# Memory norm, keys and values before the input's products, and the long convolution's tiles handed out in another order

## The chip, the core and the metric

The kernel runs on one core of one Trainium2 chip. The metric is the device time of one execution in microseconds (us). Besides it there is a profile of one execution, whose span runs from the first to the last instruction.

## The reference

Two transformer blocks are applied one after the other to 256 positions of width 1024, all in float32. Only the first part of the first block matters here.

```
h     = rmsnorm(x) * norm_mix_g                     # x: 256 x 1024
p_a, p_b, q, p_g = split(h @ w_in)                  # w_in: 1024 x 9216
y_a   = (gb * causal_conv3(gc * v)) @ w_a_out       # gb, gc, v = split(p_a)
u     = u * sigmoid(ug)                             # u, ug = split(p_b)
u     = silu(layernorm(causal_conv31(u) + bias))    # 31 taps for each of 1024 channels
y_b   = u @ w_b_out
k, vm = split((rmsnorm(mem) * norm_mem_g) @ w_kv)   # mem: 256 x 1024, w_kv: 1024 x 2048
y_c   = attention(q, k, vm) @ w_att_out             # 4 heads of 256
out   = (sigmoid(p_g0)*y_a + sigmoid(p_g1)*y_b + sigmoid(p_g2)*y_c) @ w_o
```

The feed-forward part and the whole second block follow. They are the same in both kernels.

## The kernel before

Everything is one program with five instruction streams, each written out by hand and each executed in its order: SyncE (weight loads), GpSimd, ScalarE, VectorE and TensorE. They meet only at counted semaphores.

**Slots.** A weight matrix is read in pieces of 1 MB (128 x 2048 float32). A piece is here called a slot. Each is split into an upper and a lower part: ScalarE copies `raw` to `whi` (line 489, the helper `hi`), VectorE subtracts, `wlo = raw - whi` (line 843, the helper `lo`), and TensorE multiplies in three passes (line 1317): upper by upper, upper by lower, lower by upper. There are three buffers (`R = 3`), so slot g+3 can be loaded when `lo(g)` is done, and `hi(g+3)` can run when TensorE has used slot g (`slot_used`). TensorE starts slot g when `lo(g)` is done (`lo_ready`).

**Stages of the first 345 us.** Slots 0 to 11 are `ugq` (u, its gate ug and the attention's queries q, three slots a round, four rounds), 12 to 19 are `kv` (four slots of keys by `to_channels`, four of values by `to_rows`), 20 to 31 are `cvb` (for branch a, four rounds of three), 32 to 43 are `gate` (four rounds of three), and 44 on are `a_out`. Below, u1 to u12, kv1 to kv8, c1 to c12 and g1 to g12 are the slots of these stages in order. The variable `G_KV` and its like hold the first slot of a stage. `USES` counts how often each of the eight PSUM banks was read before a stage.

**Norms.** A norm takes squares on ScalarE (line 499), statistics on VectorE and GpSimd, a scaling on VectorE (line 862), 16 transposes on TensorE (line 1364, which write PSUM banks 0 to 3), and the split of the result (ScalarE `norm_upper`, VectorE `norm_lower`). `n_mix` is the norm of `x`, `n_mem` that of `mem`. Before, `n_mix` comes first, and `n_mem` runs during `ugq`; its transposes and split stand between `ugq` and `kv`. There too stand three transposes of `cwf_rows`, copied out by ScalarE (line 594).

**The long convolution.** Its eight tiles of 128 channels are shared: VectorE does tiles 0 to 5, GpSimd tiles 6 and 7. VectorE's share of a tile is cut into four parts of 7 or 8 taps (line 965, one instruction a tap; a first part has two copies more, a last part one addition). The parts stand between the `lo` of the slots: before, two in round 2 and two in round 3 of `ugq` (tile 0), one behind each `lo` of `kv` (tiles 1 and 2), one in each round of `cvb` (tile 3), two in each round of `gate` (tiles 4 and 5). Tile c can begin when round c//2 of `ugq` has given u (`glu`). GpSimd takes two instructions a tap (lines 426 and 430), 31 taps a tile, and begins when both norms are transposed (`norm_tr` is 8), since its scratch is the norms' buffer `xn`, and when `glu` says that tiles 6 and 7 are there.

**A round of `cvb` on VectorE** (`branch_a`): a product (line 1003), a `lo`, the three-tap convolution (lines 1014 and 1017), a `lo`, a product (line 1022), and then a `lo` whose `hi` stands on ScalarE behind a copy of that product's result (line 616):

```
                act.wait_ge(bank_read[2], USES["cvb"][2] + 1 + i)
                nc.scalar.activation(q_hi[:, bass.ds(BW * i, BW)], work[:, 1860:2372], ACT.Copy).then_inc(an_hi, 1)
                hi(G_CVB + 5, i)
```

Then a lower part (line 1025) and the round's part of the long convolution follow.

Of the kernel before, what the change touches and what calls it, by code (L numbers as in the profile page):

```python
# [18 lines left out]
ACT = mybir.ActivationFunctionType  # L19
# [14 lines left out]
CONV_DVE = 6  # L34
# [22 lines left out]
G_UGQ, G_KV, G_CVB, G_GATE, G_AO, G_ATT, G_BO, G_WO = 0, 12, 20, 32, 44, 48, 52, 56  # L57
# [15 lines left out]
    ("setup", {0: 1}), ("n_mix", LOW4), ("ugq", {1: 4, 2: 4}), ("setup2", {3: 1}), ("n_mem", LOW4),  # L73
    ("kv", {**LOW4, **HIGH4}), ("cvb", {0: 4, 1: 4, 2: 4}), ("gate", {0: 4, 1: 4, 2: 4}),
# [22 lines left out]
NORMS = ["n_mix", "n_mem", "n_ffn", "fin1", "n_mix2a", "n_ffn2a", "n_mix2b", "n_ffn2b", "fin2"]  # L97
TNORMS = ["n_mix", "n_mem", "n_ffn", "n_mix2a", "n_ffn2a", "n_mix2b", "n_ffn2b"]
TGAIN = [V_MIX, V_MEM, V_FFN, V_MIX2, V_FFN2, V_MIX2 + 1, V_FFN2 + 1]


def two_blocks(nc, d, out):
    with ExitStack() as ctx:
# [176 lines left out]
        def _(sp):  # L280
            x_rows = d["x"].rearrange("(t p) n -> p t n", p=P)
            for t in range(T):
                sp.dma_start(x[:, t, :], x_rows[:, t, :]).then_inc(x_in[t], 16)

# [14 lines left out]
            for j, c0 in enumerate((3 * D, 4 * D, 5 * D)):  # L299
                load(G_UGQ + j, cols("w_in", c0), KD)  # L300
            with sp.Fori(1, 4) as i:
                for j, c0 in enumerate((3 * D, 4 * D, 5 * D)):
                    load(G_UGQ + j, cols("w_in", c0 + 256 * i), KD, i)
            for i in range(4):
                load(G_KV + i, cols("w_kv", 256 * i), KD)
            for i in range(4):
                load(G_KV + 4 + i, d["w_kv"].rearrange("(k p) n -> p k n", p=P)[:, 2 * i:2 * i + 2, D:2 * D], 2)
# [53 lines left out]
        def _(pool):  # L361
# [55 lines left out]
            for c in range(CONV_DVE, KD):  # L417
                pool.wait_ge(glu, 2 + c // 2)
                dst = conv[:, c * S:(c + 1) * S]
                for k in range(K_B):  # L420
                    src, w = misc[:, c * UP + k:c * UP + k + S], gain(V_CONVB + k, c)
                    if k == 0:
                        nc.gpsimd.tensor_scalar(dst, src, w, gain(V_CBIAS, c), ALU.mult, ALU.add).then_inc(pool_tap, 1)
                    else:
                        tap = xn[:, 0, S * (k % 2):S * (k % 2) + S]
                        nc.gpsimd.tensor_scalar(tap, src, w, None, ALU.mult).then_inc(pool_mul, 1)  # L426
                        steps += 1
                        pool.wait_ge(pool_mul, steps)
# [50 lines left out]
        def _(act):  # L479
# [89 lines left out]

            act.dma_start(vec_rows, d["vecs"]).then_inc(vec_in, 16)  # L570
            act.dma_start(mem_rows, d["mem"].rearrange("(t p) n -> p t n", p=P)).then_inc(mem_in, 16)
            squares("n_mix", x, lambda b: act.wait_ge(x_in[b // 2], 16))
# [4 lines left out]
            norm_upper("n_mix", p_hi)  # L577
# [3 lines left out]
            squares("n_mem", mem_rows, lambda b: act.wait_ge(mem_in, 16))  # L581
# [11 lines left out]
            act.wait_ge(vec_tr, 2)  # L593
            nc.scalar.activation(cwf[:, :], bank(3, 0, K_F * FT), ACT.Copy).then_inc(bank_read[3], 1)
            norm_upper("n_mem", q_hi)

            for i in range(4):
                act.wait_ge(slot_used, G_KV + i + 1)
                nc.scalar.activation(kreg[:, BW * i:BW * (i + 1)], bank(i), ACT.Copy).then_inc(bank_read[i], 1)
                hi(G_KV + i + 3)  # L600
            for i in range(4):
                if i == 3:
                    act.wait_ge(slot_used, G_KV + 8)
                    for b in range(4):
                        nc.scalar.activation(v_tok[:, b // 2, BW * (b % 2):BW * (b % 2) + BW], bank(4 + b),
                                             ACT.Copy).then_inc(bank_read[4 + b], 1)
                hi(G_KV + 7 + i)

# [226 lines left out]
        def _(dve):  # L835
# [106 lines left out]
            normalise("n_mix", x)  # L942
            norm_lower("n_mix", p_hi, p_lo)
            lo(0)
            lo(1)
            lo(2)

# [25 lines left out]
            def ugq(i, parts=()):  # L973
# [7 lines left out]
                for part in parts[:1]:  # L981
                    conv_part(0, 0, part, 2)
                lo(G_UGQ + 5, i)
                for part in parts[1:]:
                    conv_part(0, 0, part, 2)

            ugq(0)
            normalise("n_mem", mem_rows)
            ugq(1, (0, 1))
            ugq(2, (2, 3))  # L990
            ugq(3)
            norm_lower("n_mem", q_hi, q_lo)
# [35 lines left out]
            for i in range(4):  # L1028
                branch_a(i)
                conv_part(3, 3 * TAPS, i, 3)  # L1030
            for i in range(4):
                for j in range(3):
                    lo(G_GATE + 3 + j, i)
                    if j:
                        c = 4 + i // 2
                        conv_part(c, c * TAPS, 2 * (i % 2) + j - 1, 4)
# [274 lines left out]
        def _(pe):  # L1311
# [145 lines left out]
            transpose_norm("n_mix")  # L1457
            phases = (("ugq", G_UGQ), ("cvb", G_CVB), ("gate", G_GATE))

            def memory():  # L1460

                pe.wait_ge(cwf_in, 16)
                for k in range(K_F):
                    last = nc.tensor.transpose(bank(3, FT * k, FT * (k + 1)), cwf_rows[:, P * k:P * k + P],
                                               ident[0:FT, 0:FT])
                last.then_inc(vec_tr, 1)
                pe.wait_ge(glu, 5)
                transpose_norm("n_mem")
                for i in range(4):
                    free(i, USES["kv"][i])  # L1470
                    to_channels(G_KV + i, i, q_pair, 0, "n_mem" if i == 0 else None)
                for i in range(4):
                    to_rows(G_KV + 4 + i, 2, q_pair, 2 * i, 4, 2, BW, i == 0, i == 3)
# [23 lines left out]
            pe.wait_ge(conv_tap, (K_B + 3) * CONV_DVE)  # L1497
            pe.wait_ge(pool_tap, K_B * (KD - CONV_DVE))
# [195 lines left out]
```

## Time and profile before

| | us |
|---|---|
| time, median of 3 runs | 1332.91 (1332.78 to 1339.92) |
| span of the profiled execution | 1326.9 |
| median of the runs less that span | 6.0 |
| TensorE busy in the span | 1207.3 (91%) |
| VectorE busy | 856.2 (65%) |
| ScalarE busy | 619.5 (47%) |
| GpSimd busy | 310.5 (23%) |
| weight split on VectorE (line 843), 189 instructions | 440.2 |
| taps on VectorE (line 965), 174 instructions | 89.9 |

The profiled execution has no time of its own beside its span. Busy shares are means over stages with different limits, so a stage is read from its own rows: which engine the others wait for, and for how long. In a row of the timeline, the numbers are the start, the length, the engine, the line, the operation and the tiles; the bracket at the end is the idle time ahead of it and what ended that. "x8" is eight instructions, drawn as one.

### The profile page before, as it was taken

The numbers are of one execution on the slowest core, as the hardware profiler recorded it, in microseconds if no ns is written. First come the engines' busy times: TensorE is split into PE (matmuls) and PEld (weight loads), VectorE is DVE, ScalarE is ACT, GpSimd is POOL, SyncE is SP. The second block draws the span as 40 slices with busy tenths as digits, with TensorE's granted clock in tenths as the row PEclk, the third lists the DMA queues.
The fourth block names the chain that finished last, engine by engine and source line by source line (L and its number), as shares of the span: only waits on it lengthen the run. The fifth ranks groups of instructions, "written<-read, shape, count | busy, mean of one in ns | idle before, by whom it ended". The sixth has DMA issues, their size and how long they took to land.

```text
span 1326.9 us, 20560 instructions
## 1 busy us (share of the span) xinstructions
PE 1207.3 (91%) x8039; PEld 1116.8 (84%) x8039; DVE 856.2 (65%) x1099; ACT 619.5 (47%) x834; POOL 310.5 (23%) x301
## 2 busy tenths in 40 slices
PE   5989899999799899999677889999989988899997
PEld 5989789999798899998566769999979777799996
DVE  4678988887566666667568846555554485655554
ACT  5553323444444444444457634444444474444442
POOL 1009999601300100000113405870000140000000
PEclk8999999999799899999888899999999979999999
DMA  8553444555136455554233027555545502355550
GB/s 261 176 184 115 140 151 154 189 190 190 32 128 192 150 190 188 180 181 147 83 131 127 1 96 200 188 190 190 190 128 189 190 1 94 129 191 190 185 189 37
DMA packets 139431, 201.00 MB, mean 151 GB/s; under 512 B 3258, under 2 KB 119994, under 8 KB 139376
## 3 DMA queue, kind: packets, MB, share of 16 engines
q1 hardware_dynamic: 138128, 195.83, 44.9%
q0 software_dynamic: 912, 3.17, 1.1%
q10 hardware_dynamic: 336, 1.25, 0.3%
q8 instruction: 36, 0.59, 0.2%
q14 instruction: 19, 0.16, 0.0%
HBM read 199.19 MB, written 1.05 MB: 151 GB/s over the span
## 4 chain that ended last, share of the span: by engine, by line
PE 74%; DVE 17%; ACT 5%; issue 2%; POOL 1%; DMA 1%; POOLq 0%; ACTq 0%; SPq 0%
PE ps L1317 68%; DVE wlo L843 5%; DVE work L965 4%; PE ps L1378 4%; ACT whi L489 2%; ACT xn L499 1%; PE ps L1364 1%; PE ps L1414 1%; DVE work L926 1%; DVE work L1017 1%; ACT p_hi L509 1%; DMA x<-in_x 1%; DVE stat L916 1%; POOL q_lo L383 0%; DVE x L884 0%
## 5 line engine op out<-in xcount | busy, mean ns | idle before, releaser
L843 DVE TENSOR_TENSOR wlo<-raw,whi 128x2048 fp32r<-128x2048 f32 x189 | 440.2, 2332 | 248.7 <-ACT whi L489 248.3
L1317 PE MATMUL ps<-p_hi,whi 128*128 128x256 f32 x1632 | 467.6, 287 | 21.5 <-DVE wlo L843 17.6
L1317 PE MATMUL ps<-p_lo,whi 128*128 128x256 f32 x1632 | 465.8, 285 | 0.0
L1317 PE MATMUL ps<-p_hi,wlo 128*128 128x256 f32 x1632 | 465.5, 285 | 0.0
L489 ACT ACTIVATE whi<-raw 128x2048 fp32r<-128x2048 f32 x189 | 361.3, 1914 | 187.0 <-PE ps L1317 187.0
L1317 PEld LDWEIGHTS ps<-p_hi,whi 128*128 128x128 f32 x1632 | 317.1, 194 | 26.7 <-DVE wlo L843 19.9
L1317 PEld LDWEIGHTS ps<-p_lo,whi 128*128 128x128 f32 x1632 | 317.2, 194 | 1.5
L1317 PEld LDWEIGHTS ps<-p_hi,wlo 128*128 128x128 f32 x1632 | 317.2, 194 | 0.0
L377 POOL TENSOR_TENSOR stat<-stat 128x1 f32<-128x1 f32 x18 | 14.8, 822 | 647.1 <-DVE stat L851 647.1
L1317 PE MATMUL ps<-whi,q_hi 128*128 128x512 f32 x376 | 148.0, 394 | 3.6 <-DVE wlo L843 2.0
L1317 PE MATMUL ps<-whi,q_lo 128*128 128x512 f32 x376 | 147.6, 392 | 0.0
L1317 PE MATMUL ps<-wlo,q_hi 128*128 128x512 f32 x376 | 146.8, 390 | 0.0
L965 DVE SCALAR_TENSOR_TENSOR work<-work 128x256 f32<-128x256 f32 x174 | 89.9, 586 | 0.0
L1317 PEld LDWEIGHTS ps<-whi,q_hi 128*128 128x128 f32 x376 | 71.1, 189 | 18.9 <-DVE wlo L843 2.9
L1317 PE MATMUL ps<-whi,p_hi 128*128 128x512 f32 (+2 forms) x196 | 77.0, 393 | 10.6 <-DVE p_lo L1188 3.9
L426 POOL TENSOR_SCALAR xn<-misc,vec 128x256 f32<-128x256 f32 x60 | 85.5, 1425 | 0.0
L1317 PEld LDWEIGHTS ps<-wlo,q_hi 128*128 128x128 f32 x376 | 71.0, 189 | 15.2
L1317 PEld LDWEIGHTS ps<-whi,q_lo 128*128 128x128 f32 x376 | 71.2, 189 | 13.2
L1317 PE MATMUL ps<-wlo,p_hi 128*128 128x512 f32 (+2 forms) x196 | 76.4, 390 | 0.0
L1317 PE MATMUL ps<-whi,p_lo 128*128 128x512 f32 (+2 forms) x196 | 76.3, 389 | 0.0
L779 ACT ACTIVATE work<-ps 128x512 f32<-128x512 f32 x32 | 19.1, 597 | 120.0 <-PE ps L1317 120.0
L430 POOL TENSOR_TENSOR misc<-misc,xn 128x256 f32<-128x256 f32 x60 | 64.5, 1075 | 5.0
(209 smaller groups left out, 1560.2 us busy)
## 6 DMA issues: line engine op xcount, KB each, us to landing
raw<-in_w_in SPq DMA_DIRECT2D x36, 1024.0 KB, 5.0
raw<-in_w_up SPq DMA_DIRECT2D x22, 1024.0 KB, 5.1
raw<-in_up_a SPq DMA_DIRECT2D x16, 1024.0 KB, 5.4
raw<-in_down_a SPq DMA_DIRECT2D x16, 1024.0 KB, 4.9
raw<-in_up_b SPq DMA_DIRECT2D x16, 1024.0 KB, 5.4
raw<-in_down_b SPq DMA_DIRECT2D x16, 1024.0 KB, 4.9
raw<-in_od_w_qkv SPq DMA_DIRECT2D x12, 1024.0 KB, 5.1
raw<-in_w_down SPq DMA_DIRECT2D x11, 1024.0 KB, 4.9
```

The source lines that it names most:

```text
L377: nc.gpsimd.tensor_tensor(out=rr[:, c:c + 1], in0=ms[:, c:c + 1], in1=mhalf[:, 0:1], op=ALU.pow).then_inc(norm_r, 1)
L426: nc.gpsimd.tensor_scalar(tap, src, w, None, ALU.mult).then_inc(pool_mul, 1)
L430: nc.gpsimd.tensor_tensor(out=dst, in0=dst, in1=tap, op=ALU.add).then_inc(pool_tap, 1)
L489: nc.scalar.activation(whi[:, g % R, :], raw[:, g % R, :], ACT.Copy).then_inc(hi_ready, 1)
L499: last = nc.scalar.activation(xn[:, t, half], src[:, t, half], ACT.Square, accum_out=ss[:, T * n + t, m:m + 1])
L509: nc.scalar.activation(dst[:, c * S:(c + 1) * S], bank(c // 2, c % 2 * S, c % 2 * S + S), ACT.Copy, scale=gain(TGAIN[m], c)).then_inc(norm ...
L779: nc.scalar.activation(work[:, 0:BW], bank(slot), ACT.Relu).then_inc(f2_r, 1)
L843: nc.vector.tensor_tensor(wlo[:, g % R, :], raw[:, g % R, :], whi[:, g % R, :].bitcast(F32), ALU.subtract).then_inc(lo_ready, 1)
L916: nc.vector.tensor_scalar(att_nmax[:, pair], att_max[:, pair], -1.0 if biased else -scale(i), None, ALU.mult).then_inc(at_nm, 1)
L965: nc.vector.scalar_tensor_tensor(out=acc[k % 2], in0=src, scalar=w, in1=acc[k % 2], op0=ALU.mult, op1=ALU.add).then_inc(conv_tap, 1)
L1317: ins = nc.tensor.matmul(dst, lhs, rhs, start=first and n == 0, stop=last and n == 2)
L1378: ins = nc.tensor.matmul(dst, a, b, start=first and n == 0, stop=last and n == 2)
```

## The change

The memory's part comes first. SyncE loads three slots of `w_kv`, then `x`, then the rest of `w_kv`, and only then `w_in`; ScalarE's queue loads `mem` ahead of the vectors. The first norm is `n_mem`, slots 0 to 7 are `kv`, and 8 to 19 are `ugq`. The norm of `x` is computed during kv1 to kv4, and its transposes stand behind kv4, with those of `cwf_rows` ahead of them. `cvb` and `gate` keep their slot numbers 20 to 43.

The convolution's tiles are handed out anew: GpSimd takes tiles 0 and 1, VectorE tiles 2 to 7. VectorE's 24 parts are taken from a list in order: one in round 2 of `ugq`, three each in rounds 3 and 4, two in each round of `cvb`, and one behind each of the first nine `lo` of `gate`. None stands in `kv`.

```diff
-CONV_DVE = 6
+CONV_POOL = 2
...
-G_UGQ, G_KV, G_CVB, G_GATE, G_AO, G_ATT, G_BO, G_WO = 0, 12, 20, 32, 44, 48, 52, 56
+G_KV, G_UGQ, G_CVB, G_GATE, G_AO, G_ATT, G_BO, G_WO = 0, 8, 20, 32, 44, 48, 52, 56
...
         @block.sync
-            for t in range(T):
-                sp.dma_start(x[:, t, :], x_rows[:, t, :]).then_inc(x_in[t], 16)
...
-            for j, c0 in enumerate((3 * D, 4 * D, 5 * D)):
-                load(G_UGQ + j, cols("w_in", c0), KD)
-            with sp.Fori(1, 4) as i:
+            for i in range(3):
+                load(G_KV + i, cols("w_kv", 256 * i), KD)
+            for t in range(T):
+                sp.dma_start(x[:, t, :], x_rows[:, t, :]).then_inc(x_in[t], 16)
+            load(G_KV + 3, cols("w_kv", 256 * 3), KD)
+            for i in range(4):
+                load(G_KV + 4 + i, d["w_kv"].rearrange("(k p) n -> p k n", p=P)[:, 2 * i:2 * i + 2, D:2 * D], 2)
+            with sp.Fori(0, 4) as i:
                 for j, c0 in enumerate((3 * D, 4 * D, 5 * D)):
                     load(G_UGQ + j, cols("w_in", c0 + 256 * i), KD, i)
...
         @block.gpsimd
             pool.wait_ge(norm_tr, 8)
-            for c in range(CONV_DVE, KD):
+            for c in range(CONV_POOL):
                 pool.wait_ge(glu, 2 + c // 2)
...
         @block.scalar
             def squares(name, src, ready=None):
                 n = NORMS.index(name)
+                if name == "n_mix":
+                    act.wait_ge(norm_tr, 4 * TNORMS.index("n_mem") + 4)
...
+            act.dma_start(mem_rows, d["mem"].rearrange("(t p) n -> p t n", p=P)).then_inc(mem_in, 16)
             act.dma_start(vec_rows, d["vecs"]).then_inc(vec_in, 16)
-            act.dma_start(mem_rows, d["mem"].rearrange("(t p) n -> p t n", p=P)).then_inc(mem_in, 16)
-            squares("n_mix", x, lambda b: act.wait_ge(x_in[b // 2], 16))
+            squares("n_mem", mem_rows, lambda b: act.wait_ge(mem_in, 16))
...
-            norm_upper("n_mix", p_hi)
+            norm_upper("n_mem", q_hi)
             hi(0)
             hi(1)
             hi(2)
-            squares("n_mem", mem_rows, lambda b: act.wait_ge(mem_in, 16))
+            squares("n_mix", x, lambda b: act.wait_ge(x_in[b // 2], 16))
+            for i in range(4):
+                act.wait_ge(slot_used, G_KV + i + 1)
+                nc.scalar.activation(kreg[:, BW * i:BW * (i + 1)], bank(i), ACT.Copy).then_inc(bank_read[i], 1)
+                hi(G_KV + i + 3)
+            act.wait_ge(vec_tr, 2)
+            nc.scalar.activation(cwf[:, :], bank(3, 0, K_F * FT), ACT.Copy).then_inc(bank_read[3], 1)
+            norm_upper("n_mix", p_hi)
+            for i in range(4):
+                if i == 3:
+                    act.wait_ge(slot_used, G_KV + 8)
+                    for b in range(4):
+                        nc.scalar.activation(v_tok[:, b // 2, BW * (b % 2):BW * (b % 2) + BW], bank(4 + b),
+                                             ACT.Copy).then_inc(bank_read[4 + b], 1)
+                hi(G_KV + 7 + i)
...
         @block.vector
-            normalise("n_mix", x)
-            norm_lower("n_mix", p_hi, p_lo)
+            normalise("n_mem", mem_rows)
+            norm_lower("n_mem", q_hi, q_lo)
             lo(0)
             lo(1)
             lo(2)
+            normalise("n_mix", x)
+            for i in range(4):
+                lo(G_KV + 3 + i)
+            norm_lower("n_mix", p_hi, p_lo)
+            for i in range(4, 8):
+                lo(G_KV + 3 + i)
...
+            parts_left = [(c, part) for c in range(CONV_POOL, KD) for part in range(4)]
+
+            def conv_parts(count):
+                for _ in range(count):
+                    c, part = parts_left.pop(0)
+                    conv_part(c, (c - CONV_POOL) * TAPS, part, 2 + c // 2)
+
+            def ugq(i, count):
                 lo(G_UGQ + 3, i)
...
                 lo(G_UGQ + 4, i)
-                for part in parts[:1]:
-                    conv_part(0, 0, part, 2)
+                conv_parts(count // 2)
                 lo(G_UGQ + 5, i)
-                for part in parts[1:]:
-                    conv_part(0, 0, part, 2)
-
-            ugq(0)
-            normalise("n_mem", mem_rows)
-            ugq(1, (0, 1))
-            ugq(2, (2, 3))
-            ugq(3)
-            norm_lower("n_mem", q_hi, q_lo)
-            for i in range(8):
-                lo(G_KV + 3 + i)
-                conv_part(1 + i // 4, TAPS * (1 + i // 4), i % 4, 3)
+                conv_parts(count - count // 2)
+
+            ugq(0, 0)
+            ugq(1, 1)
+            ugq(2, 3)
+            ugq(3, 3)
...
             for i in range(4):
                 branch_a(i)
-                conv_part(3, 3 * TAPS, i, 3)
+                conv_parts(2)
             for i in range(4):
                 for j in range(3):
                     lo(G_GATE + 3 + j, i)
-                    if j:
-                        c = 4 + i // 2
-                        conv_part(c, c * TAPS, 2 * (i % 2) + j - 1, 4)
+                    conv_parts(min(len(parts_left), 1))
...
         @block.tensor
             last.then_inc(vec_tr, 1)
+            transpose_norm("n_mem")
+            phases = (("ugq", G_UGQ), ("cvb", G_CVB), ("gate", G_GATE))
+
+            for i in range(4):
+                free(i, USES["kv"][i])
+                to_channels(G_KV + i, i, q_pair, 0, "n_mem" if i == 0 else None)
+            free(3, USES["setup2"][3])
+            pe.wait_ge(cwf_in, 16)
+            for k in range(K_F):
+                last = nc.tensor.transpose(bank(3, FT * k, FT * (k + 1)), cwf_rows[:, P * k:P * k + P],
+                                           ident[0:FT, 0:FT])
+            last.then_inc(vec_tr, 1)
             transpose_norm("n_mix")
...
+            for i in range(4):
+                to_rows(G_KV + 4 + i, 2, q_pair, 2 * i, 4, 2, BW, i == 0, i == 3)
             ready_low("n_mix")
...
                 if phase == "cvb":
-                    memory()
+                    pe.wait_ge(glu, 5)
```

## Rows read from the trace of the kernel before

**Rows 1.** busy time of each engine in two stretches, us from the start

```profile
core 0: us, PE busy (x) PEld busy (x) DVE busy (x) ACT busy (x) POOL busy (x), PEclk, DMA share, GB/s
98.00:147.00 49.00, 46.93 (x287) 42.01 (x288) 42.52 (x56) 16.48 (x15) 47.25 (x43) 0.97 0.38 129
147.00:231.00 84.00, 74.37 (x580) 72.73 (x580) 76.14 (x93) 28.09 (x23) 81.41 (x64) 0.96 0.46 150
```

**Rows 2.** chain of work that ended last: start, length, what

```profile
20.53 71.28 PE ps L1317 x576
...
97.99 6.12 PE ps L1317 x48
...
250.18 70.87 PE ps L1317 x576
```

**Rows 3.** TensorE in order of time: the first product after a wait

```profile
147.96 0.38 PE L1317 MATMUL ps<-p_hi,whi 128*128 128x256 f32 x1 [0.52 <-DVE wlo L843]
...
211.26 0.39 PE L1317 MATMUL ps<-p_hi,whi 128*128 128x256 f32 x1 [2.46 <-DVE wlo L843]
...
230.66 0.38 PE L1317 MATMUL ps<-p_hi,whi 128*128 128x256 f32 x1 [0.39 <-DVE wlo L843]
...
250.18 0.58 PE L1317 MATMUL ps<-p_hi,whi 128*128 128x256 f32 x1 [1.99 <-DVE wlo L843]
```

**Rows 4.** VectorE in order of time, rounds of the `cvb` loop

```profile
168.43 2.28 DVE L843 TENSOR_TENSOR wlo<-raw,whi 128x2048 fp32r<-128x2048 f32 x1
...
188.95 2.27 DVE L843 TENSOR_TENSOR wlo<-raw,whi 128x2048 fp32r<-128x2048 f32 x1
...
203.51 4.89 DVE L965 SCALAR_TENSOR_TENSOR work<-work 128x256 f32<-128x256 f32 x8
...
208.93 2.28 DVE L843 TENSOR_TENSOR wlo<-raw,whi 128x2048 fp32r<-128x2048 f32 x1
...
216.27 0.68 DVE L1022 TENSOR_TENSOR work<-ps,work 128x512 f32<-128x512 f32 x1
...
219.55 2.29 DVE L843 TENSOR_TENSOR wlo<-raw,whi 128x2048 fp32r<-128x2048 f32 x1 [2.60 <-ACT whi L489]
...
228.33 2.28 DVE L843 TENSOR_TENSOR wlo<-raw,whi 128x2048 fp32r<-128x2048 f32 x1
```

**Rows 5.** VectorE in order of time, GpSimd idle (first row) and working

```profile
63.05 3.25 DVE L965 SCALAR_TENSOR_TENSOR work<-work 128x256 f32<-128x256 f32 x8
...
121.94 2.84 DVE L843 TENSOR_TENSOR wlo<-raw,whi 128x2048 fp32r<-128x2048 f32 x1
...
139.96 0.30 DVE L955 COPY work<-misc 128x286 f32<-128x286 f32 x1
...
145.63 2.28 DVE L843 TENSOR_TENSOR wlo<-raw,whi 128x2048 fp32r<-128x2048 f32 x1
```

**Rows 6.** GpSimd in order of time: first and last of its taps

```profile
96.83 0.55 POOL L423 TENSOR_SCALAR misc<-misc,vec 128x256 f32<-128x256 f32 x1 [50.30 <-PE ps L1364]
...
98.37 0.74 POOL L430 TENSOR_TENSOR misc<-misc,xn 128x256 f32<-128x256 f32 x1
...
100.10 0.73 POOL L430 TENSOR_TENSOR misc<-misc,xn 128x256 f32<-128x256 f32 x1
...
253.12 0.73 POOL L430 TENSOR_TENSOR misc<-misc,xn 128x256 f32<-128x256 f32 x1
```

**Rows 7.** ScalarE in order of time: the start, the pace of the slots

```profile
8.33 0.63 ACT L499 ACTIVATE xn<-x 128x512 f32<-128x512 f32 x1 [1.41 <-DMA x<-in_x]
...
28.48 1.91 ACT L489 ACTIVATE whi<-raw 128x2048 fp32r<-128x2048 f32 x1 [1.22 <-PE ps L1317]
...
126.94 1.92 ACT L489 ACTIVATE whi<-raw 128x2048 fp32r<-128x2048 f32 x1 [3.12 <-PE ps L1317]
...
132.38 1.92 ACT L489 ACTIVATE whi<-raw 128x2048 fp32r<-128x2048 f32 x1 [3.52 <-PE ps L1317]
```

**Rows 8.** the tile `merged`, which the load of `mem` writes

```profile
L571 ACTq DMA_DIRECT2D merged<-in_mem x1: 443/443/443, 1.2 to 1.2; - x1
...
DMA to landing us min/median/max: 9.3/9.3/9.3
```

More of the change, by code:

```diff
@@ L72 @@
 PHASES = [
-    ("setup", {0: 1}), ("n_mix", LOW4), ("ugq", {1: 4, 2: 4}), ("setup2", {3: 1}), ("n_mem", LOW4),
-    ("kv", {**LOW4, **HIGH4}), ("cvb", {0: 4, 1: 4, 2: 4}), ("gate", {0: 4, 1: 4, 2: 4}),
+    ("setup", {0: 1}), ("n_mem", LOW4), ("kv", {**LOW4, **HIGH4}), ("setup2", {3: 1}), ("n_mix", LOW4),
+    ("ugq", {1: 4, 2: 4}), ("cvb", {0: 4, 1: 4, 2: 4}), ("gate", {0: 4, 1: 4, 2: 4}),
     ("a_out", LOW4), ("att1", {2: 2, 3: 2, **HIGH4}), ("att_out", LOW4), ("b_out", LOW4),
@@ L95 @@
 USES = earlier_bank_uses()
-NORMS = ["n_mix", "n_mem", "n_ffn", "fin1", "n_mix2a", "n_ffn2a", "n_mix2b", "n_ffn2b", "fin2"]
-TNORMS = ["n_mix", "n_mem", "n_ffn", "n_mix2a", "n_ffn2a", "n_mix2b", "n_ffn2b"]
-TGAIN = [V_MIX, V_MEM, V_FFN, V_MIX2, V_FFN2, V_MIX2 + 1, V_FFN2 + 1]
+NORMS = ["n_mem", "n_mix", "n_ffn", "fin1", "n_mix2a", "n_ffn2a", "n_mix2b", "n_ffn2b", "fin2"]
+TNORMS = ["n_mem", "n_mix", "n_ffn", "n_mix2a", "n_ffn2a", "n_mix2b", "n_ffn2b"]
+TGAIN = [V_MEM, V_MIX, V_FFN, V_MIX2, V_FFN2, V_MIX2 + 1, V_FFN2 + 1]
 def two_blocks(nc, d, out):
@@ L297, in rows @@
                 return d[w].rearrange("(k p) n -> p k n", p=P)[:, bass.ds(k0, kk), :]
-            for j, c0 in enumerate((3 * D, 4 * D, 5 * D)):
-                load(G_UGQ + j, cols("w_in", c0), KD)
-            with sp.Fori(1, 4) as i:
+            for i in range(3):
[6 more added lines that the diff above has]
+            with sp.Fori(0, 4) as i:
                 for j, c0 in enumerate((3 * D, 4 * D, 5 * D)):
                     load(G_UGQ + j, cols("w_in", c0 + 256 * i), KD, i)
[L304 to L307, printed above, removed]
             with sp.Fori(1, 5) as i:
@@ L592, in _ @@
                 hi(G_UGQ + 5, i)
[L593 to L607, printed above, removed]
             with act.Fori(0, 4) as i:
@@ L971, in conv_part @@
                         in1=acc[1], op0=ALU.add, op1=ALU.add).then_inc(conv_tap, 1)
-            def ugq(i, parts=()):
+            parts_left = [(c, part) for c in range(CONV_POOL, KD) for part in range(4)]
[4 more added lines that the diff above has]
+            def ugq(i, count):
                 lo(G_UGQ + 3, i)
@@ L1456, in _ @@
             last.then_inc(vec_tr, 1)
-            transpose_norm("n_mix")
[L1458 to L1473, printed above, removed]
+            transpose_norm("n_mem")
[9 more added lines that the diff above has]
+            last.then_inc(vec_tr, 1)
+            transpose_norm("n_mix")
+            for i in range(4):
+                to_rows(G_KV + 4 + i, 2, q_pair, 2 * i, 4, 2, BW, i == 0, i == 3)
             ready_low("n_mix")
@@ L1496, in _ @@
                 to_channels(G_AO + i, i, q_pair)
[L1497 to L1498 removed]
+            pe.wait_ge(conv_tap, (K_B + 3) * (KD - CONV_POOL))
+            pe.wait_ge(pool_tap, K_B * CONV_POOL)
             free(7, USES["att1"][7])
```

## The prediction

> **What bounds the kernel now.** I read the busy times by stretch first. From 98 to 147 us (`kv`) and from 147 to 231 us (`cvb`) TensorE is busy nearly throughout, but VectorE is too: 42.5 of 49 and 76.1 of 84 us, with GpSimd at 47 of 49 and 81 of 84 [rows 1]. Which of the two leads is told by the chain of waits. It runs through TensorE alone from 20.53 us for 12 slots of `ugq` (71.28 us) and again from 250.18 us for 12 slots (g4 to the third of `a_out`, 70.87 us) [rows 2]. Between 97.99 and 250 us it runs mostly through VectorE. TensorE's own rows agree: its waits there end with a `wlo` of VectorE, 2.46 us ahead of c10 and 1.99 us ahead of g4 [rows 3].
>
> TensorE's pace when nothing holds it: slot u1 takes 20.53 to about 28.45 (ScalarE's copy for the next one starts at 28.48 [rows 7]), 7.9 us, and the other eleven 5.77 each [rows 2]. A row slot of `kv` takes 132.38 - 126.94 = 5.44 us [rows 7]. A round of three slots is 17.3 us.
>
> VectorE's pace in a round of `cvb` is the distance of its first `wlo`: 168.43, 188.95, 208.93, 228.33, that is 20.52, 19.98 and 19.40 us [rows 4]. In each stands one part of the long convolution. Beside GpSimd's work a part of 8 taps takes 4.85 us (203.51 to 208.4 [rows 4]) and a first part 5.67 us (139.96 to 145.63 [rows 5]). Without the part the rounds are 14.85, 15.1 and 14.55, mean 14.85. This holds 2.6 us in which VectorE waits for ScalarE (216.27 + 0.68 to 219.55 [rows 4]); what stands behind that wait can't fill it. So a `cvb` round is over TensorE's 17.3 us already with one part.
>
> **What the change does to it.** Neither the 44 slots nor the 24 parts on VectorE nor the 62 taps on GpSimd change in number. Only their places do: 4, 8, 4 and 8 parts in `ugq`, `kv`, `cvb` and `gate` become 7, 0, 8 and 9. I follow the new order from the start, with the durations above.
>
> Start. The first squares now want `mem`. Before, the second half of `x` let them start at 8.33 [rows 7]; `mem` was issued at 1.2 us and took 9.3 us beside `x` and the vectors [rows 8]. It goes first now, but all four squares (two of 0.63 us more) come behind it. Below: nothing, if it lands in the time of half a load. Above: issued at 0.7, it lands at 10.0, 1.7 us later than `x`, plus 1.3 of squares: 3 us. It has the lead over only the 1 MB of `w_kv`, so I take 0.5: TensorE starts at 21.0.
>
> `kv`. Slots kv1 to kv4: 7.9 + 3 x 5.77, to 46.2 us. Then bank 3 must be copied, a `hi` stands ahead of the copy of the `cwf` transposes, and the 16 transposes of `n_mix` follow. Before, the same chain and the lower split made TensorE go from 91.8 to 97.99 [rows 2], 6.2 us. The split is no longer waited for; I take 4.4 (ends: 3 and 6.2). Its cover is that `wlo` of kv5 to kv7 are done by then, and that the norm's squares, statistics and scaling run beside kv1 to kv4, where VectorE has 2.3 of each 5.8 us to do. kv5 to kv8 are 21.7 us: `ugq` starts at 72.3. Before, `kv` was paced by VectorE (a `lo` of 2.75 and a part of 4.85 make 7.6 us a slot).
>
> `ugq`. u1 to u10 run at 5.77, u11 and u12 too. GpSimd starts when round 1 gives u, about 14.2 us in, at 86.5 (before 96.83 [rows 6]). The parts: `lo(u9)` ends at 111.7, the first part at 117.4, `lo(u10)` 119.9, the product for u and `lo(u11)` 124.7, a part 129.5, `lo(u12)` 132.3, two parts 142.0, `lo(c1)` 144.6, the last product of u 145.3. TensorE has used u12 at 141.5 and waits for that product ahead of `cvb`: c1 starts at 145.3. Before it started at 147.96 [rows 3]. That is the whole gain: 2.7 us.
>
> `cvb`. VectorE goes on: `lo(c2)` 148.0, a first part 153.7, `lo(c3)` 156.4, two parts 166.1, the product 166.7, `lo(c4)` 169.0. TensorE, done with c3 at 162.6, starts c4 there. From c4 to c7 to c10 to g1 VectorE has 14.85 us and two parts each: 4.9 + 5.7, 4.85 + 4.85, 4.9 + 5.7. The sum is 25.45 + 24.5 + 25.45 = 75.4 us, against 3 x 17.3 on TensorE. g1 starts at 244.4. Before it was 230.66 [rows 3]. `cvb` takes 99.1 us from c1 to g1 instead of 82.7.
>
> `gate`. GpSimd's taps took 96.83 to 253.85, 157 us [rows 6]; from 86.5 on they end near 241 to 244, just as g1 starts. From there a part costs 3.25 [rows 5] and a `lo` 2.2. The last `cvb` round then needs from `lo(g1)` on: 2.7 of taps of branch a, 2.2, 0.7, 2.6 of waiting, 2.2, 1.0, two parts 6.4, and `lo(g4)` 2.2: 20.0 us, g4 at 264.4 (before 250.18). After that a slot costs VectorE 5.5 us on the mean, less than 5.77, so TensorE leads. Its 12 slots take 69.6 us (before 70.87, behind a longer wait), to 334.0. Before they ended at 250.18 + 70.87 = 321.05.
>
> Sum: -2.7 to c1, +16.4 in `cvb`, +0.5 in g1 to g3, -1.3 in the 12 slots: +12.9 us. From there on everything is as before. Against the profiled span that is 1326.9 + 12.9 = 1339.8; the median of the runs lies 6.0 above the span, so 1332.9 + 12.9 = 1345.8, say 1346 us, 1.0% more.
>
> The waits of 6 to 7 us ahead of c4, c7, c10 and g1 may also leave TensorE at its lower clock for the first slot behind them, as in u1 (7.9 for 5.77). This costs nothing: a round has 25 us for 17.3 + 2.1.
>
> The price of a part beside GpSimd is the term that matters. The row says that 8 taps go from 3.25 to 4.89 us [rows 4, 5], and a `wlo` from 2.29 to 2.84. The Trainium skill ("SBUF — State Buffer", section "SBUF: two separate sides") states instead that VectorE with two SBUF inputs and GpSimd lock a shared pair of ports for a whole instruction and the other fully blocks. By that rule a tap of 0.41 us would stand behind a GpSimd instruction of 0.73 or more each time, 1.14 us, and a part would cost 9.1 us; the four added in `cvb` would cost 36 us instead of 19.8. The trace does not agree for these forms: its part takes 4.89.
>
> **Rivals.** (a) *VectorE is relieved in time; faster.* GpSimd's tap step is 1.73 us where VectorE is idle (98.37 to 100.10 [rows 6]), 107 us for 62. In the new order VectorE is nearly idle until 111.7. If GpSimd were done near its 107 us, at 194, the two last long rounds would cost 1.6 us less for each part and some 1.5 less for the rest, about 4.7 each, the contended half round before it some 2, and the last parts of `cvb` too: 11 to 12 us back and g1 at 233, and with contention cheaper in rounds 1 and 2 besides (7 us at most) the time would be 1326 to 1334. Its point of decision: GpSimd's end must be before about 195 us. Against it: 157 - 107 = 50 us of its time were lost beside VectorE's instructions, and all but the first 25 us lie beside just such work. Chance 0.05.
>
> (b) *Part of this only; no change or little.* GpSimd ends near 225, or the parts fill waits better than I think, and 6 to 10 us come off: 1336 to 1340. For it: the free start. Chance 0.13, half of it within 0.5%.
>
> (c) *The change does not move the bound.* If `ugq` and `cvb` were paced by TensorE all the same, the end would come from 72.3 + 36 x 5.77 = 280.0 + 17.3 = 297.4 instead of 321.05: 1309 us. Against it are the 19.4 us rounds with a single part. Chance 0.02.
>
> (d) *`gate` stays behind.* If GpSimd lasts to 260, the last `cvb` round and the first five `gate` slots stay at 7.0 to 7.6 us each: 5 + 5 to 8 us more, 1353 to 1358. For it: two parts a round meet it longer. Chance 0.1.
>
> (e) *The start and the break behind kv4 cost their upper ends*: 2.5 + 1.8 us more, 1350. This lies in my forecast's own range.
>
> (f) *The lock.* 13 parts beside GpSimd at 4.3 us more than now: 1400. The row of before, which holds 12 such parts, speaks against it: chance 0.01.
>
> **How the numbers follow.** My forecast has 0.69: own range 1341 to 1352, from the terms that I rounded (start and break -1.5 to +4.3, GpSimd's end by 10 us earlier -3, the base of a round 14.55 to 15.1, so -1 to +1). A measurement of this kernel can tell some 0.5%, 6.7 us, from no change, that is 1326.2 to 1339.6. Faster: (c) and half of (a), with a little for what I can't see, 0.06. Same: the rest of (a) and half of (b), 0.09. Slower: 0.85. The range that leaves out (a), (c), (f) and the far parts of (b) and (d): 1337 to 1354.
>
> **What would show it.** Right: `kv` from 21 to 72 us without a wait but one of some 4 us behind its fourth slot; GpSimd's first tap at 86 and its last near 242; VectorE's first `wlo` of a `cvb` round 24.5 to 25.5 us apart; TensorE waiting 6 to 8 us for it each time, four times; no long wait behind g4; a first score near 334. Wrong: rounds under 22 us, which would mean that a part is cheap beside GpSimd or that GpSimd is done; waits on `wlo` deep in `gate` (rival d); a later start than 23; or a change behind 345 us, which none of my steps allows.

## The result, and the profile after

| | before | changed |
|---|---|---|
| time, median | 1334.4 us (4 runs) | 1350.6 us (1347.3 to 1355.2, 4 runs) |
| ratio, 95% interval | | 1.0122, 1.0064 to 1.0180 |
| span of the profiled execution | 1326.9 | 1349.1 |
| third slot of `a_out` ends | 321.05 | 335.30 |

The change makes the kernel 1.2% slower. The second timing, below, gives 1.0099 (1.0071 to 1.0127). Both intervals leave out 1, and both lie below 2%. The forecast was 1346 us.

Busy time by stretch. These answer to [rows 1]:

```profile
core 0: us, PE busy (x) PEld busy (x) DVE busy (x) ACT busy (x) POOL busy (x), PEclk, DMA share, GB/s
98.00:147.00 49.00, 46.42 (x387) 46.22 (x386) 38.66 (x43) 26.55 (x20) 47.33 (x41) 1.00 0.45 150
148.00:246.00 98.00, 77.16 (x576) 76.35 (x576) 90.04 (x119) 24.36 (x18) 91.20 (x77) 0.87 0.39 129
```

In `cvb` VectorE is busy 90 of 98 us and TensorE 77. Before, the two were nearly level there (76 and 74 of 84). TensorE now plainly waits. The chain of what ended last, against [rows 2]:

```profile
0.74 7.59 DMA merged<-in_mem
...
21.81 25.28 PE ps L1319 x192
...
49.93 3.35 PE ps L1366 x16
...
53.28 68.12 PE ps L1319 x480
...
246.30 89.00 PE ps L1319 x720
```

The load of `mem` lands at 8.3 us, after which all four squares run; TensorE starts at 21.81. Behind kv4 the 16 transposes take 3.35 us. From 53.28 TensorE leads for twelve slots (four of `kv`, eight of `ugq`), and from 246.30 for fifteen, to 335.30. Between them lies VectorE. TensorE's waits, against [rows 3]:

```profile
148.52 0.38 PE L1319 MATMUL ps<-p_hi,whi 128*128 128x256 f32 x1 [4.10 <-DVE misc L989]
...
171.13 0.58 PE L1319 MATMUL ps<-p_hi,whi 128*128 128x256 f32 x1 [3.59 <-DVE wlo L841]
...
196.24 0.58 PE L1319 MATMUL ps<-p_hi,whi 128*128 128x256 f32 x1 [5.22 <-DVE wlo L841]
...
221.26 0.58 PE L1319 MATMUL ps<-p_hi,whi 128*128 128x256 f32 x1 [5.65 <-DVE wlo L841]
...
246.30 0.58 PE L1319 MATMUL ps<-p_hi,whi 128*128 128x256 f32 x1 [6.17 <-DVE wlo L841]
```

The first is c1, which waits 4.1 us for the last product of u. The others are c4, c7, c10 and g1: a wait each round, 3.6 to 6.2 us. There is none from g1 to the third slot of `a_out`. VectorE in `cvb`, against [rows 4]:

```profile
168.81 2.27 DVE L841 TENSOR_TENSOR wlo<-raw,whi 128x2048 fp32r<-128x2048 f32 x1
...
193.91 2.28 DVE L841 TENSOR_TENSOR wlo<-raw,whi 128x2048 fp32r<-128x2048 f32 x1
...
207.90 10.18 DVE L969 SCALAR_TENSOR_TENSOR work<-work 128x256 f32<-128x256 f32 x16
...
218.60 2.60 DVE L841 TENSOR_TENSOR wlo<-raw,whi 128x2048 fp32r<-128x2048 f32 x1
...
230.37 2.29 DVE L841 TENSOR_TENSOR wlo<-raw,whi 128x2048 fp32r<-128x2048 f32 x1 [2.60 <-ACT whi L487]
...
243.97 2.28 DVE L841 TENSOR_TENSOR wlo<-raw,whi 128x2048 fp32r<-128x2048 f32 x1
```

The first `wlo` of a round come at 168.81, 193.91, 218.60 and 243.97: 25.1, 24.7 and 25.4 us apart, where they were 19.4 to 20.5. Two parts stand in each round; 16 taps take 10.18 us, 0.64 each. The wait of 2.60 us for ScalarE is still there. GpSimd, against [rows 6]:

```profile
89.75 0.55 POOL L421 TENSOR_SCALAR misc<-misc,vec 128x256 f32<-128x256 f32 x1 [61.92 <-DVE misc L989]
...
241.65 0.72 POOL L428 TENSOR_TENSOR misc<-misc,xn 128x256 f32<-128x256 f32 x1
```

Its taps go from 89.75 to 242.4, 153 us, and so cover all of `cvb` but its last 4 us.

### The profile page after: what moved, and what is told of

The parts are those of the page before. It is cut to its first block, busy times and chain, and to the rows that moved or that the text cites. A ratio compares the mean times of both kernels' runs of the same rounds, so it can differ in the third digit from the quotient of the medians.

```text
span 1349.1 us, 20583 instructions
## 1 busy us (share of the span) xinstructions
PE 1222.3 (91%) x8039; PEld 1133.2 (84%) x8039; DVE 852.5 (63%) x1099; ACT 620.4 (46%) x834; POOL 306.5 (23%) x301
## 4 chain that ended last, share of the span: by engine, by line
PE 77%; DVE 14%; ACT 5%; issue 2%; DMA 1%; POOL 1%; POOLq 0%; ACTq 0%
PE ps L1319 70%; PE ps L1380 4%; DVE work L969 4%; DVE wlo L841 3%; ACT whi L487 2%; PE ps L1416 1%; PE ps L1366 1%; ACT xn L499 1%; DVE work L924 1%; DMA merged<-in_mem 1%; DVE work L1021 1%; DVE stat L911 0%; DVE stat L914 0%; DVE x L882 0%; DVE p_lo L867 0%
## 5 line engine op out<-in xcount | busy, mean ns | idle before, releaser
L1319 PE MATMUL ps<-p_hi,whi 128*128 128x256 f32 x1632 | 469.6, 288 | 29.0 <-DVE wlo L841 20.6
L1319 PEld LDWEIGHTS ps<-wlo,q_hi 128*128 128x128 f32 x376 | 70.7, 188 | 15.1
L1276 DVE TENSOR_TENSOR work<-work 128x512 f32<-128x512 f32 x32 | 22.8, 712 | 67.1 <-ACT work L777 67.1
```

The lines of the kernel that those rows point to most:

```text
L1276: nc.vector.tensor_tensor(work[:, 1024:1536], work[:, 0:BW], work[:, 0:BW], ALU.mult).then_inc(f2_sq, 1)
L1319: ins = nc.tensor.matmul(dst, lhs, rhs, start=first and n == 0, stop=last and n == 2)
```

## The experiments

Each is the kernel before or the changed one with the edit shown. "Third of `a_out`" is where the chain of waits puts the end of that slot; it tells what the first 345 us did and leaves out what follows. Medians and ratios are against the kernel before on the same chip. Its own runs went from 1321.5 to 1340.6 us, so a single span says little and the ratio counts.

| kernel | order | third of `a_out` | span | median | ratio (95%) |
|---|---|---|---|---|---|
| before | input first | 321.1 | 1326.9 | 1334 to 1336 | 1 |
| changed, again | memory first | 334.4 | 1347.3 | 1348.2 | 1.0099 (1.0071 to 1.0127) |
| tiles only | input first | 318.6 | 1330.6 | 1336.4 | 1.0011 (0.9984 to 1.0037) |
| parts to gate | memory first | 322.3 | 1328.2 | 1334.9 | 1.0012 (0.9988 to 1.0035) |
| part in the wait | memory first | 324.7 | 1334.5 | 1339.2 | 1.0040 (1.0015 to 1.0066) |
| part in the wait | input first | 313.6 | 1332.0 | 1330.6 | 0.9942 (0.9915 to 0.9970) |
| both, GpSimd kept | memory first | 315.3 | 1329.2 | 1331.2 | 0.9974 (0.9955 to 0.9994) |
| no GpSimd taps, work left out | memory first | 307.3 | 1315.3 | 1322.9 | 0.9923 (0.9890 to 0.9955) |
| all tiles on VectorE | memory first | 300.1 | 1312.2 | 1314.9 | 0.9860 (0.9832 to 0.9888) |
| all tiles on VectorE | input first | 307.4 | 1309.4 | 1321.0 | 0.9904 (0.9882 to 0.9927) |
| same, norm not held up | input first | 300.5 | 1312.6 | 1313.4 | 0.9825 (0.9780 to 0.9870) |

**1. The tiles handed out anew, alone.** The old order; GpSimd takes tiles 0 and 1, and VectorE's parts are taken from the list at their old places.

```diff
-            for c in range(CONV_DVE, KD):
+            for c in range(CONV_POOL):
                 pool.wait_ge(glu, 2 + c // 2)
...
-                conv_part(1 + i // 4, TAPS * (1 + i // 4), i % 4, 3)
+                conv_parts(1)
```

> Old order of stages, but the tiles handed out as in the change: GpSimd 0 and 1, VectorE 2 to 7, the parts at their old places. My theory (the loss is in where the parts stand, not in who does which tile): no change against the kernel before, 1333 us within 4, GpSimd's first tap again near 97 us, because it still waits for both norms' transposes. Rival (the hand-out itself costs): 5 us or more slower, with waits of TensorE in ugq or kv that were not there.

No difference that can be told (1.0011, interval 0.9984 to 1.0037). GpSimd's first tap is again at 96.85 us. So who does which tile is not the loss.

**2. Four parts moved from cvb.**

```diff
-            ugq(1, 1)
+            ugq(1, 2)
...
                 branch_a(i)
-                conv_parts(2)
+                conv_parts(1)
```

> The changed kernel with 2, 3 and 3 parts in ugq (was 1, 3, 3), one part in each cvb round (was two) and twelve in gate (was nine). My theory: cvb rounds of 19.5 to 20.5 us instead of 25; the first gate slot near 225 us instead of 246; no new wait in gate, where a slot has 5.77 us for 2.2 + 3.25; the third slot of a_out ends near 313 us (335 in the changed kernel, 321 in the one before), so 8 us faster than the kernel before, 1325. Rival (GpSimd's work reaches into gate and twelve parts there are too many): gate slots of 7 us, nothing gained over the kernel before, 1333 or more.

```profile
149.28 0.57 PE L1319 MATMUL ps<-p_hi,whi 128*128 128x256 f32 x1 [5.13 <-DVE misc L989]
...
171.88 0.39 PE L1319 MATMUL ps<-p_hi,whi 128*128 128x256 f32 x1 [3.69 <-DVE wlo L841]
...
192.50 0.39 PE L1319 MATMUL ps<-p_hi,whi 128*128 128x256 f32 x1 [1.60 <-DVE wlo L841]
...
212.47 0.39 PE L1319 MATMUL ps<-p_hi,whi 128*128 128x256 f32 x1 [2.44 <-DVE wlo L841]
```

The rounds fall to 20.6 and 20.0 us, and the waits at c7 and c10 to 1.6 and 2.4. The third of `a_out` comes at 322.3, 13 us earlier than in the changed kernel, so the doubled parts of `cvb` are the loss. It comes 9 us later than I expected (313). c4 still starts at 171.9: that place is set by the parts of `ugq`'s last round, which this edit leaves alone, and I had wrongly counted a part off there. In `gate` there is one wait of that size, 2.0 us at g4: GpSimd works until 249.2 us here, into `gate`, as the rival had it. All in all the time is that of the kernel before (1334.9), equal and not 8 us faster. This is the number that the rival named. The theory held for the rounds of `cvb`, not for what lies on either side of them.

**3. GpSimd's taps left out.** Tiles 0 and 1 of the convolution are set to zero.

```diff
             for c in range(CONV_POOL):
                 pool.wait_ge(glu, 2 + c // 2)
-                dst = conv[:, c * S:(c + 1) * S]
...
+                nc.gpsimd.memset(conv[:, c * S:(c + 1) * S], 0.0).then_inc(pool_tap, 1)
```

> The changed kernel, in which GpSimd writes zeros to tiles 0 and 1 instead of their 62 taps (those two tiles of the convolution are left out). My theory (what a part costs beside GpSimd is a third of its price): parts of 3.25 us, cvb rounds of 20 to 21 us instead of 25, first gate slot near 221 us, 24 us less than the changed kernel, 1326. Rival (the taps are slow in this stage for another reason, such as the moved loads): rounds stay at 24 to 25, 1350.

```profile
179.60 0.38 PE L1306 MATMUL ps<-p_hi,whi 128*128 128x256 f32 x1 [0.36 <-DVE wlo L828]
...
199.14 0.39 PE L1306 MATMUL ps<-p_hi,whi 128*128 128x256 f32 x1 [2.01 <-DVE wlo L828]
...
218.96 0.39 PE L1306 MATMUL ps<-p_hi,whi 128*128 128x256 f32 x1 [2.29 <-DVE wlo L828]
...
237.91 0.39 PE L1306 MATMUL ps<-p_hi,whi 128*128 128x256 f32 x1 [1.40 <-DVE wlo L828]
```

With the same parts at the same places on VectorE, 16 taps take 6.42 us, TensorE waits for VectorE neither at c1 nor at c4 (the first wait is 0.36 us, at c7), and the next rounds are 19.5, 19.8 and 19.0 us. The third of `a_out` is 28 us earlier (307.3). So beside GpSimd's taps VectorE's own work is dearer, by more than the 24 us that I expected. What GpSimd takes off VectorE is not in this run, since nobody does those two tiles; experiment 6 has both.

**4 and 5. A part in the wait for ScalarE**, in the memory-first order (the changed kernel) and in the input-first order (the kernel of experiment 1).

```diff
                 nc.vector.tensor_tensor(ca, bank(2), ca, ALU.mult).then_inc(bank_read[2], 1)
+                conv_parts(1)
                 lo(G_CVB + 5, i)
...
                 branch_a(i)
-                conv_parts(2)
+                conv_parts(1)
```

(In the input-first kernel the round's single part is the one that moves.)

> The changed kernel with one of the two parts of each cvb round put between the product of line 1026 and the lo behind it, where VectorE waits 2.6 us for ScalarE. My theory (that wait is part of VectorE's round): the wait goes, rounds of 22.4 us instead of 25.0, 10 us off over four rounds, 1340. Rival (the wait only moves, or TensorE then waits for the later lo of the third slot): rounds stay above 24, 1347 to 1350.

```profile
192.60 0.39 PE L1320 MATMUL ps<-p_hi,whi 128*128 128x256 f32 x1 [1.98 <-DVE wlo L841]
...
213.76 0.58 PE L1320 MATMUL ps<-p_hi,whi 128*128 128x256 f32 x1 [2.14 <-DVE wlo L841]
...
236.12 0.38 PE L1320 MATMUL ps<-p_hi,whi 128*128 128x256 f32 x1 [3.33 <-DVE wlo L841]
```

Rounds of 21.8, 21.2 and 22.4 us, 10.6 us less at the third of `a_out` than in the changed kernel, and a median of 1339.2: as expected.

> Old order, tiles handed out as in the change, GpSimd with its two tiles, and only the part of each cvb round moved into the wait for ScalarE. My theory: rounds of 17.3 to 17.6 us (TensorE's) instead of 19.4 to 20.5, the first gate slot near 223 us instead of 231, 7 to 9 us off, 1325 to 1328. Rival (the wait moves elsewhere): rounds above 19, 1333.

Rounds of 17.6 us: 186.94, 204.54 and 222.14 are VectorE's `wlo`. Behind c4 TensorE has no wait of 0.25 us or more in these stages. The third of `a_out` is 7.4 us earlier than in the kernel before, and 5.0 earlier than in experiment 1, which differs from this one by the moved parts alone. The time falls by 0.6%, to 1330.6, where I had expected 1325 to 1328. The 2.6 us wait was part of every round.

**6. All eight tiles on VectorE, both orders.** The tap loop of GpSimd is taken out, `CONV_POOL = 0`, 32 parts.

```diff
-            ugq(0, 0)
-            ugq(1, 1)
+            ugq(0, 2)
+            ugq(1, 3)
...
-                    conv_parts(min(len(parts_left), 1))
+                    conv_parts(2 if i == 0 and j == 0 else 1)
```

> The changed order of stages with the same two edits: VectorE does all eight tiles (11 parts in ugq, 8 in cvb, one of each round's two in the wait, 13 in gate), GpSimd none. My theory (the order itself is worth nothing either way once VectorE is not the bound): the third slot of a_out ends within 4 us of the old order with the same edits, 300 to 306, 1312 to 1319. Rival (memory first gives VectorE too little room, since eight slots have no part beside them): waits on wlo in ugq and cvb, 8 us or more behind the old order's kernel.

```profile
53.02 247.09 PE ps L1304 x1968
```

```profile
core 0: us, PE busy (x) PEld busy (x) DVE busy (x) ACT busy (x) POOL busy (x), PEclk, DMA share, GB/s
148.00:246.00 98.00, 98.00 (x819) 98.00 (x818) 97.74 (x172) 40.24 (x35) 0.00 (x0) 1.00 0.54 177
```

From 53.02 us the chain is one piece of TensorE, 247 us for 43 slots: four row slots at 5.44 and 39 at 5.77 are 246.8. VectorE is busy for 97.7 of 98 us in the middle and is waited for nowhere. 1.4% faster than the kernel before, 2.4% faster than the changed one, with a third more taps on VectorE.

VectorE's busy time from the start to the end of the third slot of `a_out`, in the kernel before (24 parts) and in this one (32 parts, memory first):

```profile
core 0: us, DVE busy (x), PEclk, DMA share, GB/s
0.00:321.05 321.05, 252.48 (x323) 0.97 0.53 174
...
0.00:300.11 300.11, 243.20 (x391) 0.99 0.56 184
```

With 62 taps more, VectorE is busy for 9 us less; input first, in the next two kernels, it is 243.7 and 243.1. Time that an instruction stands behind GpSimd counts as busy. So GpSimd's share costs VectorE more than it takes off it.

> Old order of stages; GpSimd does no tile of the long convolution, VectorE does all eight (32 parts: 8 in ugq, 8 in kv, 4 in cvb, 12 in gate), and in cvb the part stands in the wait for ScalarE. My theory (GpSimd's 62 taps cost VectorE more than they save it): parts of 3.25 us and wlo of 2.29 throughout, nearly every slot at TensorE's 5.77, the third slot of a_out ends near 299 to 303 us (321 in the kernel before), 1311 to 1317, faster than before by 1.2 to 1.6%. Rival (eight more parts are too much for VectorE, the split of work is worth its contention): waits on wlo in kv and gate, 1333 or more.

```profile
104.60 0.55 PE L1304 MATMUL ps<-q_hi,whi 128*128 128x256 f32 x1 [8.23 <-DVE q_lo L853]
```

Faster than before, but neither theory: the third of `a_out` is 307.4, not 299 to 303, and nothing waits in `kv` or `gate`. The loss is one wait of 8.2 us ahead of kv1. The two parts behind the last `lo` of `ugq` stand ahead of the memory norm's lower part on VectorE, and kv1 needs that.

**7. The same without parts in ugq's last round.**

```diff
-            ugq(3, 3)
+            ugq(3, 0)
...
                 branch_a(i)
+                conv_parts(min(i, 1))
```

> As the old order with all eight tiles on VectorE, but with no part in the last round of ugq and three more in cvb (5 in ugq, 8 in kv, 7 in cvb, 12 in gate), so that VectorE is free when the memory norm's lower part is due between ugq and kv. There TensorE waited 8.2 us with three parts in that round. My theory (the old order's weak place is that break, where the norm's last step stands on the path, and a part there comes straight on top): kv starts near 98 us again, the third slot of a_out ends 6 to 7 us earlier than with three parts there, near 297 to 299 us, and the two orders of stages are equal within 3 us, 1312 to 1316. Rival (the memory-first order is itself better, by its shorter break and nothing else in the way): 4 us or more remain behind the changed order's kernel, 1318 or more.

```profile
97.87 202.64 PE ps L1305 x1584
```

kv1 starts at 97.87 and TensorE leads to 300.5, within 0.4 us of the memory-first kernel. It is 6.9 us earlier than in the kernel with three parts there, as expected; the median is 1313.4. The intervals of the ratios, 0.9825 and 0.9860, overlap. Where VectorE is not the bound, the order of the stages is worth nothing that can be told. The order does matter in what can stand between the stages: input first, a part in the wrong place holds up a norm.

**8. Everything but GpSimd's share.** Memory first, 8 parts in `ugq`, one in each `cvb` round in the wait, 12 in `gate`, GpSimd with tiles 0 and 1.

```diff
             for c in range(CONV_POOL):
                 pool.wait_ge(glu, 2 + c // 2)
...
+            ugq(1, 2)
...
+                conv_parts(1)
                 lo(G_CVB + 5, i)
```

> The changed order with GpSimd's two tiles kept and both other repairs: 8 parts in ugq, one in each cvb round and that in the wait for ScalarE, 12 in gate. My theory (what is left against the kernel without GpSimd's taps is contention): cvb rounds of 17.3 to 17.6 us from c4 on, but c4 still near 171 (it is set by ugq's last parts), gate slots of 7 us until GpSimd ends near 245 to 250, the third slot of a_out near 313 to 317, 1326 to 1330, so 12 or more behind the kernel with all tiles on VectorE. Rival (only the places were wrong, GpSimd is no burden): within 5 us of it, 1320 or less.

The `cvb` rounds are 17.9, 17.6 and 17.6 us. The third of `a_out` is at 315.3 (57.85 us of TensorE behind a last wait at 257.49), and the median 1331.2. That slot is 15 us behind the kernel with all tiles on VectorE, which does 62 taps more there. So the places are worth 20 us against the changed kernel (335.3 to 315.3), and GpSimd's work costs another 15 with the parts at these places.

GpSimd lasts until 254.2 us, longer than expected. c4 starts at 172.6. With all tiles on VectorE it comes near 161.3, an estimate from 53.02, four slots at 5.44 and fifteen at 5.77. So 11 of the 15 us are lost by c4, beside GpSimd and the parts of the last round of `ugq`. No run keeps GpSimd's tiles and takes parts out of that round, so the smallest cost of GpSimd's share is not known.

**9. The changed kernel again.**

> The changed kernel once more, unaltered, for a second profile. The first profile lost 14 us by 335 us, and 7 to 8 more near 1110, in the third attention, where the granted clock was low for longer. My theory (that second loss is not of the change, but differs from run to run): the loss by 335 us is again 13 to 16, the stretch from 1074 to 1124 takes another length, and the median is 1346 to 1351. Rival (the second loss belongs to the change): the same 7 to 8 us near 1110 again.

The loss by the third of `a_out` is 13.3 us (14.3 in the first profile). The third attention, from its place near 1064 to 1078 us on, over 40 us in each, in the order before, changed, changed again:

```profile
core 0: us, PE busy (x), PEclk, DMA share, GB/s
1064.00:1104.00 40.00, 34.90 (x213) 0.85 0.00 1
...
1078.00:1118.00 40.00, 38.97 (x176) 0.58 0.00 1
...
1077.00:1117.00 40.00, 36.14 (x204) 0.79 0.01 2
```

The granted clock is 0.85, 0.58 and 0.79 of full speed: a mean of its two levels, 1.2 and 2.4 GHz, in unlike shares of the time, in the same code. Against the kernel before, the first profile loses 6.2 us in this attention (15.9 us behind at its start, 22.1 at its end), the second 1.4 (17.0 and 18.4). That part of the span's difference is thus not shown to be the change's.

The same goes for everything behind the third of `a_out`. The code there is the same in all twelve profiles, and it takes from 1002.0 us (all tiles on VectorE, input first) to 1018.4 (part in the wait, input first). The kernel before has 1005.9, the changed one 1013.8 and 1012.9, the tiles alone in the old order 1012.0.

## Why the prediction was right

**The mechanism.** The loss came in `cvb`, by the step that was forecast: VectorE's rounds with two parts each. The rounds were forecast at 25.45, 24.5 and 25.45 us and are 25.1, 24.7 and 25.4. GpSimd ends at 242.4 (forecast 241 to 244), but it starts at 89.75 and not at 86.5 and takes 153 us and not 157, so two errors offset each other there. `cvb` takes 97.8 us from c1 to g1 (forecast 99.1, before 82.7).

The waits of TensorE are smaller than the 6 to 8 us that I named as a sign: 3.6, 5.2, 5.7 and 6.2. In part the time went into slots at the lower clock. In the second profile c4 to c6 ran at full clock behind a wait of 3.6 us, and the wait ahead of c7 was 7.6 us and not 5.2; c7 still started 25.1 us behind c4 in both. So in `cvb` the clock costs nothing, as forecast, and the round is VectorE's.

Experiments 2 to 5 and 8 take away each factor of it: the second part, the contention, the wait for ScalarE. Rival (a) was not met: GpSimd gains only those 4 us. Of rival (b) nothing came: GpSimd does not end near 225, and the time lies above its range. Rival (c) fell with the waits at c4 to g1. Rival (d) did not happen: GpSimd was done before `gate`, and no `wlo` was waited for there. Of rival (e) the break behind kv4 came out at its upper end, 6.2 us, and the start at 0.8 of its 2.5. Rival (f) had the wrong price: beside GpSimd a tap takes 0.60 to 0.64 us on the mean, not 1.14. But the forecast was wrong to say that the trace does not agree with the rule of the lock. The single instructions, in the last section, show one engine standing behind the other; what fails is the working that made every tap stand behind a whole GpSimd instruction.

**Sizes that were off.** (1) The break behind kv4: I took 4.4 us, it is 6.2 (47.1 to 53.28). From the end of kv4 to the first transpose it takes 2.8 us, as before (2.95). But the 16 transposes took 3.35 us, at a mean granted clock of 0.78 between 48 and 52 us; before they took 1.94, at 1.00. (2) The start: 21.81 for 21.0; `mem` landed at 8.3, in the time of `x`, but all four squares stand behind it. With both, and 0.6 us more on the way, c1 starts at 148.52 and not at 145.3: the 2.7 us that I called the whole gain are not there at all (147.96 before). (3) g1 to g3: I had VectorE set g4 20.0 us behind g1. VectorE's `wlo` for g4 was done at 265.2, 18.9 us behind g1, and TensorE did not wait for it. The fifteen slots from g1 take 89.0 us, 2.4 over 15 x 5.77, as TensorE's clock was 0.65 between 246 and 254 us. I had said that this costs nothing, with VectorE's 25 us rounds as its cover. In `cvb` that held, at g1 it did not. The forecast had 89.6 for this stretch, so its length agrees by luck. Summed: +0.6, +15.1, -1.4, so +14.3 us by the third of `a_out` where I had +12.9. c1 came 3.2 us late, `cvb` was 1.3 us shorter and the rest 0.6 shorter than forecast: part of the agreement is errors that offset each other.

**"From there on everything is as before"** is not contradicted, but the profiles can't show it to better than some us. The spans differ by 22.2 us, 14.3 of them in the first 335 us. By the forecast's own list a change behind 345 us was a sign of being wrong, and there are 7.9 us. Of these, 6.2 are in the third attention, where the second profile has 1.4. And the stretch behind the third of `a_out` differs by 16 us among kernels with the same code there (experiment 9); the kernel before lies in the lower part of that spread.

**The base.** I put 6.0 us between span and median. The changed kernel's profiled execution took 1350.87 us with a span of 1349.1, so only 1.8 us lie around a span. The profiled execution of the kernel before was then near 1328.7, a short one of its kind. By their ratios the times lie 13 to 16 us apart, which agrees with the 13.3 to 14.3 us of the first stretch better than the spans do. Some of the agreement of 1346 with 1350.6 is luck.

## What to carry to other kernels

An engine that helps can cost the engine it helps. Here GpSimd took a quarter of the taps from VectorE and gave it back in slower instructions, and 32 parts on VectorE alone ran in less time than 24 beside it, in both orders and at every placing of the parts that was tried. Before work is shared between two engines, time one instruction of each with the other idle and busy. When deferrable work is interleaved by hand, budget it round by round against what the leading engine needs in that round: a total that fits says nothing, and the cheapest place is a wait that stands in the helper's own chain.

## What the runs showed of the hardware

Beside GpSimd's tap instructions the 128x256 taps on VectorE follow each other every 0.60 to 0.64 us instead of 0.40, and a `wlo` behind taps took 2.84 us (at 121.94, [rows 5]) instead of 2.29. GpSimd suffers as well: 62 taps took 157 us before and 153 in the changed kernel. Its pace is 1.73 us a tap where VectorE does not hinder it, so they would take 107 us (an estimate). In the rows for that pace, 98.37 to 100.10 us [rows 6], VectorE is not idle, as the forecast has it: it works on the norm's lower part, which reads PSUM. The pace is the same from 100.10 to 105.27, where VectorE is idle. Single instructions of both engines in the changed kernel:

```profile
204.66 2.77 POOL L428 TENSOR_TENSOR misc<-misc,xn 128x256 f32<-128x256 f32 x1
...
208.85 0.74 POOL L428 TENSOR_TENSOR misc<-misc,xn 128x256 f32<-128x256 f32 x1
209.57 1.10 POOL L424 TENSOR_SCALAR xn<-misc,vec 128x256 f32<-128x256 f32 x1
```

```profile
208.91 0.96 DVE L969 SCALAR_TENSOR_TENSOR work<-work 128x256 f32<-128x256 f32 x1
...
209.80 0.70 DVE L969 SCALAR_TENSOR_TENSOR work<-work 128x256 f32<-128x256 f32 x1
...
210.42 0.47 DVE L969 SCALAR_TENSOR_TENSOR work<-work 128x256 f32<-128x256 f32 x1
```

In experiment 3 all 97 taps from 145.9 to 250 us take 0.47 to 0.48 us (each record runs 0.08 into the next). Here the tap that starts 0.06 us behind a GpSimd addition takes 0.96, the next 0.70 and the third 0.47, over and over. GpSimd's addition takes 0.74 us, but 2.77 beside a `wlo` of 2.29. So the slowdown is not even: an instruction stands behind one of the other engine, and two taps of three pay. The Trainium skill ("SBUF — State Buffer", section "SBUF: two separate sides") has it that whichever of the two starts first has the shared ports for its whole instruction and the other fully blocks. The trace agrees in kind. In size the first tap lost 0.49 us, and the GpSimd addition had 0.68 us left to run; whether the hold ends early or the record of GpSimd ends late, no run here shows.

TensorE's granted clock is often low behind a wait, and the longer waits of the changed kernel show it. Windows of TensorE in the changed kernel (us, busy, granted clock, DMA):

```profile
core 0: us, PE busy (x), PEclk, DMA share, GB/s
148.00:152.00 4.00, 3.48 (x19) 0.65 0.78 254
170.00:174.00 4.00, 2.87 (x13) 0.50 0.41 124
174.00:178.00 4.00, 4.00 (x26) 0.68 0.46 154
```

Behind the waits of 4.1 us (c1) and 3.6 us (c4) the mean clock is 0.65 and 0.50, and the first product of c4 takes 0.58 us instead of 0.38. In `cvb` as a whole it is 0.87. The memory-first kernel without GpSimd's taps, whose longest wait there is 2.3 us, has 1.00. But it does not follow each wait: in the second profile of the changed kernel TensorE ran at 1.00 from 170.3 to 178.3 us, behind a wait of 3.6 us at c4.
